# A gate scratch laid out in runs of 1 KB, and gate loads of whole groups into two buffers

## What is computed

```python
        s = jnp.einsum('thik,hink->thin', q, sub_keys.astype(q.dtype)).astype(jnp.float32)
        s_top, i_top = lax.top_k(s, PEER_TOPK)
...
        g = jax.nn.softmax(best_s, axis=-1)
        act = jax.nn.gelu(jnp.einsum('thkd,td->thk', u_tab[eid], tb).astype(jnp.float32), approximate=False)
        return jnp.einsum('thk,thkd->td', (g * act).astype(tb.dtype), v_tab[eid])
```

## Time and profile before

| | |
|---|---|
| median of 3 runs | 2372.03 us (2370.62 to 2372.34) |
| profiled execution, first to last instruction | 2369.0 us |
| TensorE busy | 2339.9 us, 99% |
| VectorE / ScalarE / GpSimd busy | 68% / 33% / 60% |
| DMA | 509.78 MB, mean 215 GB/s; about 320 GB/s from 1380 us on |
| span without what lies around it, against the median | 3.0 us less |

### The profile page before, as it was taken

How to read it: one execution, slowest core, us unless ns; L and a number is a source line. 1 busy time by engine, 2 the same in 40 slices (tenths; PEclk the granted TensorE clock), 3 DMA queues, 4 the chain that set the end, 5 groups by cost and what they waited for, 6 DMA issues and landing times.

```text
span 2369.0 us, 38850 instructions
## 1 busy us (share of the span) xinstructions
PE 2339.9 (99%) x14998; PEld 2182.5 (92%) x14998; DVE 1620.4 (68%) x2679; ACT 770.3 (33%) x1059; POOL 1410.0 (60%) x787
## 2 busy tenths in 40 slices
PE   9999999999999999999999999999999999999998
PEld 8999999987899999999999999999889999999997
DVE  7865444555776244097998988999477777676764
ACT  4442323432232012233343344444333333333332
POOL 5554334432445555447676756877667777777763
PEclk9999999999999999999999999999999999999999
DMA  5223222226753232247677769999988898888872
GB/s 213 79 81 135 98 98 96 100 102 222 263 170 105 87 124 93 86 140 270 230 263 240 251 199 329 320 330 325 337 319 316 318 329 317 321 314 325 319 269 76
DMA packets 207744, 509.78 MB, mean 215 GB/s; under 512 B 15856, under 2 KB 104304, under 8 KB 205168
## 3 DMA queue, kind: packets, MB, share of 16 engines
q1 hardware_dynamic: 115552, 236.75, 31.3%
q10 hardware_dynamic: 55184, 136.80, 15.6%
q0 software_dynamic: 36864, 134.23, 15.2%
HBM read 424.40 MB, written 83.32 MB: 214 GB/s over the span
## 4 chain that ended last, share of the span: by engine, by line
PE 88%; DVE 7%; DMA 2%; ACT 1%; issue 1%; POOL 0%; SPq 0%; DVEq 0%; ACTq 0%; POOLq 0%
PE ps L908 51%; PE ps L644 28%; PE ps L957 3%; DMA cxb<-parked_tiles 1%; DVE prev L1703 1%; PE ps L921 1%; PE ps L821 1%; PE ps L808 1%; PE ps L816 1%; PE ps L841 1%; PE ps L825 1%; DVE n_lo L1819 1%; DMA raw<-units 0%; DMA ug<-rows_u,eid 0%; DVE hu_lo L1532 0%
## 5 line engine op out<-in xcount | busy, mean ns | idle before, releaser
L591 POOL TENSOR_SCALAR w_hi<-raw 128x1024 fp32r<-128x1024 f32 x129 | 139.7, 1083 | 515.5 <-issue 387.4
L618 POOL TENSOR_TENSOR w_lo<-raw,w_hi 128x1024 fp32r<-128x1024 f32 x128 | 316.9, 2476 | 182.1 <-PE ps L908 181.7
L618 POOL TENSOR_TENSOR w_lo<-raw,e_hi 128x1024 fp32r<-128x1024 f32 x128 | 318.6, 2489 | 173.5 <-PE ps L908 166.4
L908 PE MATMUL ps<-g_hi,w_lo 128*128 128x448 f32 x1024 | 375.4, 367 | 0.0
L908 PE MATMUL ps<-p_hi,w_lo 128*128 128x448 f32 x1024 | 375.0, 366 | 0.0
L593 POOL TENSOR_TENSOR w_lo<-raw,w_hi 128x1024 fp32r<-128x1024 f32 x129 | 319.8, 2479 | 10.7
L644 PE MATMUL ps<-h_hi,w_hi 128*128 128x288 f32 (+2 forms) x1216 | 274.1, 307 | 1.3 <-ACT ma L1225 1.1
L644 PE MATMUL ps<-h_lo,w_hi 128*128 128x288 f32 (+2 forms) x1216 | 262.9, 298 | 0.0
L644 PE MATMUL ps<-h_hi,w_lo 128*128 128x288 f32 (+2 forms) x1216 | 262.4, 297 | 0.0
L644 PEld LDWEIGHTS ps<-h_hi,w_hi 128*128 128x128 f32 x1216 | 196.7, 189 | 26.9 <-issue 24.5
L1319 ACT ACTIVATE w_hi<-raw 128x1024 fp32r<-128x1024 f32 x128 | 135.9, 1062 | 238.5 <-PE ps L908 207.0
(11 more groups left out here) (336 smaller groups left out, 5163.5 us busy)
## 6 DMA issues: line engine op xcount, KB each, us to landing
raw<-units SPq DMA_DIRECT2D x385, 512.0 KB, 3.7
gate_scratch<-gt SPq DMA_DIRECT2D x56, 512.0 KB
activation_scratch<-ge ACTq DMA_DIRECT2D x120, 224.0 KB
abuf<-activation_scratch ACTq DMA_DIRECT2D x30, 896.0 KB, 6.2
gbuf<-gate_scratch ACTq DMA_DIRECT2D x30, 896.0 KB, 9.4
prev<-ssm_in ACTq DMA_DIRECT2D x8, 1024.0 KB, 6.8
ssm_s<-prev ACTq DMA_DIRECT2D x8, 1024.0 KB, 4.2
cxb<-parked_tiles ACTq DMA_DIRECT2D x8, 870.0 KB, 6.5
```

Source lines behind the costliest of these rows:

```text
L591: pool.tensor_scalar(w_hi[:, s, :], raw[:, r, :], 1.0, 1.0, ALU.mult, ALU.mult).then_inc(s_whi, 1)
L618: pool.tensor_tensor(w_lo[:, n % 2, :], raw[:, n % RAW, :], e_hi[m % HS_].bitcast(F32), ALU.subtract)\
L908: last = mm(accp[par], w[:, k * P:(k + 1) * P], x_[:, k, t0:t0 + ND], start=k == 0 and i == 0, stop=k == KT - 1 and i == 2)
```

## The change

The scratch becomes `[16, 128, 14, 256]` floats in place of `[32, 128, 14, 128]`: for one partition and one pair of blocks, the gates of all eight tiles of a group lie together, 1 KB in place of 512 bytes. Each store still carries 512 KB. The gates of group 0 come in one load of 1664 KB, and the last pair's copy is one instruction. From group 1 on one DMA of 1792 KB loads a group's gates, to `gbuf0` for even groups and to `gbuf1` for odd ones; `gbuf1` has one half in space that the U half's operands held, so its first load stands behind the last unit of the U half. Later ones stand at the head of a group and wait until VectorE has read the buffer's last group (`s_gr`). Loads of activations stay where they were.

```diff
--- before.py
+++ after.py
@@ -141,7 +141,7 @@
 
 def trunk(nc, xT, x_rows, units, keys, cols, heads, hist_a, hist_s, ssm_in, rows_u, rows_v,
           yT, new_a, new_s, ssm_p, ssm_s):
-    gate_dram = nc.dram_tensor("gate_scratch", [2 * NG, P, NB // 2, GI // 2 * SB], F32).ap()
+    gate_dram = nc.dram_tensor("gate_scratch", [NG, P, NB // 2, GI * SB], F32).ap()
     spill = nc.dram_tensor("parked_tiles", [N_PARK, P, T], F32).ap()
     act_dram = nc.dram_tensor("activation_scratch", [TAIL, P, ND], F32).ap()
     base = ((nc.sbuf_base + 63) // 64) * 64
@@ -319,7 +319,13 @@
         p_lo = [at("p_lo0", R1 + 4 * GI * ND, [P, GI, ND], F32R),
                 at("p_lo1", R_HT + 4 * GI * ND, [P, GI, ND], F32R)]
         abuf = at("abuf", R_XS, [P, 2, GI // 2, ND])
-        gbuf = at("gbuf", R_XS + 4 * GI * ND, [P, 2, NB // 2, GI // 2, SB])
+        gbuf0 = at("gbuf0", R_XS + 8 * GI * ND // 2, [P, NB // 2, GI, SB])
+        G_LOW, G_HIGH = R_HT + 8 * GI * ND, R_XS + 8 * GI * ND
+        G_PART = NB // 4 * GI * SB
+        assert G_LOW + 4 * G_PART <= R_RING and G_HIGH + 4 * G_PART <= R1
+        gbuf1 = at("gbuf1", G_LOW, [P, 2, (G_HIGH - G_LOW) // 4])
+        gate_parts = [gbuf0[:].rearrange("p (a b) i t -> p a b i t", a=2),
+                      gbuf1[:, :, 0:G_PART].rearrange("p a (b i t) -> p a b i t", i=GI, t=SB)]
 
         yo = at("yo", R_XS, [P, KT, TK])
 
@@ -437,6 +443,7 @@
         s_gs = [sem("gates_stored0"), sem("gates_stored1")]
         s_gc = sem("last_gates_copied")
         s_gl = [sem("gates_loaded0"), sem("gates_loaded1")]
+        s_gr = sem("gates_read")
         s_al = [sem("activations_loaded0"), sem("activations_loaded1")]
         s_as = [sem("activations_stored0"), sem("activations_stored1")]
         s_scf = sem("scores_read")
@@ -528,9 +535,9 @@
             def store_gates(B, i):
 
                 sp_.wait_ge(s_gt, 2 * B + 2)
-                gs = slice(2 * NG // GQ * i, 2 * NG // GQ * (i + 1))
+                gs = slice(NG // GQ * i, NG // GQ * (i + 1))
                 sp_.dma_start(gate_dram[gs, :, B].rearrange("g p a -> p g a"),
-                              gt[:, B % 2].rearrange("p (g i) t -> p g (i t)", g=2 * NG)[:, gs]).then_inc(s_gs[B % 2], 16)
+                              gt[:, B % 2].rearrange("p (g i) t -> p g (i t)", g=NG)[:, gs]).then_inc(s_gs[B % 2], 16)
 
             i0, i1 = (U_PEER + M_LEAD) // RAW, -(-(U_PEER + TAIL + GI) // RAW)
             with sp_.Fori(1, i0) as i:
@@ -1399,16 +1406,16 @@
                 act.dma_start(abuf[:, hb], act_dram[bass.ds((g - 1) * GI + hb * (GI // 2), GI // 2)]
                               .rearrange("m p t -> p m t")).then_inc(s_al[hb], 16)
 
-            def load_gates(g, hb, blocks=NB // 2):
-
-                act.dma_start(gbuf[:, hb, 0:blocks].rearrange("p b i t -> p b (i t)"),
-                              gate_dram[bass.ds(g * 2 + hb, 1), :, 0:blocks].rearrange("a p b i -> (a p) b i"))\
-                    .then_inc(s_gl[hb], 16)
-
-            def load_half(g, hb):
-
-                load_acts(g, hb)
-                load_gates(g, hb)
+            def load_first_gates(blocks):
+
+                act.dma_start(gbuf0[:, 0:blocks].rearrange("p b i t -> p b (i t)"), gate_dram[0, :, 0:blocks])\
+                    .then_inc(s_gl[0], 16)
+
+            def load_gates(g, par):
+
+                act.dma_start(gate_parts[par].rearrange("p a b i t -> p a (b i t)"),
+                              gate_dram[bass.ds(g, 1)].rearrange("o p (a b) i -> (o p) a (b i)", a=2))\
+                    .then_inc(s_gl[par], 16)
 
             def hi_part(g, u, par):
                 act.wait_ge(s_pm, g * GI + u + 1)
@@ -1417,14 +1424,13 @@
 
             for u in range(GI):
                 activated(TAIL + u)
-                if u < 2:
+                if u == 0:
                     B = NB // 2 - 1
                     act.wait_ge(s_gs[1 - B % 2], 16 * GQ * ((B + 1) // 2))
                     act.wait_ge(s_gs[B % 2], 16 * GQ * (B // 2))
-                    load_gates(0, u, B)
+                    load_first_gates(B)
                     act.wait_ge(s_gt, NB)
-                    act.activation(gbuf[:, u, B], gt[:, B % 2, u * (GI // 2):(u + 1) * (GI // 2), :], ACT.Copy)\
-                        .then_inc(s_gc, 1)
+                    act.activation(gbuf0[:, B], gt[:, B % 2, 0:GI, :], ACT.Copy).then_inc(s_gc, 1)
                 if u:
                     hi_part(0, u - 1, 0)
                 if u == 5:
@@ -1432,12 +1438,13 @@
                     act.wait_ge(s_as[1], 8 * TAIL)
                     act.wait_ge(s_gs[B % 2], 16 * GQ * (B // 2 + 1))
                     act.wait_ge(s_p, GI // 2)
-                    load_half(1, 0)
+                    load_acts(1, 0)
+            load_gates(1, 1)
             hi_part(0, GI - 1, 0)
             act.wait_ge(s_ud, N_PICK)
             act.activation(dots[:], dots[:], ACT.Gelu).then_inc(s_act, 1)
             act.wait_ge(s_p, GI)
-            load_half(1, 1)
+            load_acts(1, 1)
 
             def group(g, par, load, i=None):
                 g0 = par if i is not None else g
@@ -1446,9 +1453,12 @@
                     if u + 1 < GI:
                         hi_part(g, u + 1, par)
                     expert_hi(NKEYS + (g0 - 1) * GI + u + HS_, i, 4)
+                    if load and u == 0:
+                        act.wait_ge(s_gr, g)
+                        load_gates(g + 1, 1 - par)
                     if load and u % 4 == 2:
                         act.wait_ge(s_p, g * GI + u + 2)
-                        load_half(g + 1, u // 4)
+                        load_acts(g + 1, u // 4)
 
             group(1, 1, True)
             with act.Fori(1, NG // 2 - 1) as i:
@@ -2027,12 +2037,15 @@
                     dve.wait_ge(s_accf[m % 2], m // 2 + 1)
                 elif u % 4 == 0:
                     dve.wait_ge(s_al[u // 4], g * 16)
-                if u % 4 == 0:
-                    dve.wait_ge(s_gl[u // 4], g * 16 + 16)
+                if u == 0:
+                    dve.wait_ge(s_gl[g % 2], g // 2 * 16 + 16)
                     if g == 0:
-                        dve.wait_ge(s_gc, u // 4 + 1)
-                v = abuf[:, u // 4, u % 4, :].rearrange("p (n t) -> p n t", t=SB)
-                tt_(v, v, gbuf[:, u // 4, :, u % 4, :], ALU.mult).then_inc(s_pm, 1)
+                        dve.wait_ge(s_gc, 1)
+                v = abuf[:, u // 4, u % 4, :].rearrange("p (a n t) -> p a n t", a=2, t=SB)
+                tt_(v, v, gate_parts[g % 2][:, :, :, u, :], ALU.mult).then_inc(s_pm, 1)
+                if u == GI - 1:
+                    dve.wait_ge(s_pm, i + 1)
+                    dve.sem_inc(s_gr, 1)
 
             def expert_low(i):
                 g, u = divmod(i, GI)
```

## The result

The changed kernel takes **2385.55 us** (median of 4 runs, 2383.95 to 2385.93) against 2371.32 (4 runs, 2370.41 to 2372.34): ratio 1.0053, 95% interval 1.0039 to 1.0066. It is slower, by 14 us where 3 were forecast, and outside the stated range. In a later measurement, on another chip, the same change came to 1.0028 (1.0017 to 1.0040), 7.5 us (experiment 8). Both intervals say slower; why the two numbers differ is only partly known (experiments 8, 12 and 14). Two executions that ran far longer than all others, 2847.85 us of the kernel before and 7677.64 us of experiment 14, are left out of all numbers here.

The account below looks back on a forecast made before the run. TensorE, busy 99% of the span, was taken as the bound, with 7.2 us at most to regain. The terms -0.3 + 1.1 + 0.7 + 1.6 = +3.1 us on 2372.0 gave 2375.1 us, range 2369.5 to 2379.0 us (8 in 10).

Parts of the forecast that it names:

- Stores, -0.3: Gate stores in 1 KB runs: less DMA time while gates are stored, worth -0.3 us (0 to -0.7).
- I take half of that back: While gates are stored: half of TensorE's 0.7 us loss counted as regained through the longer store runs.
- Pause 1, +1.1: TensorE's wait before unit 124: group 0's one long load makes the weights of m = 125 later, +1.1 us (-1.1 to +2.5).
- Rows 10 show one run per turn: DMA queues: busy queues take turns run by run, so a longer gate load holds up the weights.
- Pause 2, -0.9: First V unit's wait for a low part of group 0: ends at about 1730.6 us in place of 1731.48, -0.9 us.
- Gates of group 1: Head of group 1: one later load of all its gates lands at 1736.4 us; +0.7 us, pause 2 included.
- 9.1 us: Time from issue to landing of group 1's single gate load, from a median of 9.7 us in the trace.
- From there to TensorE's start is the old 3.50 us: Pause 3, third V unit: TensorE starts a fixed 3.50 us after VectorE's first multiplication, at 1739.9 us.
- clearly slower: Rival at the change of halves: gates of both groups land later, 6 us lost, 2378 us; chance 0.21.
- One more half-clock stretch, +1.6: Behind pause 3: TensorE idle for 3.0 us, then one more stretch at half clock, +1.6 us (0 to 1.7).
- The rest, at nothing: V half: gates asked for seven tiles ahead are hidden, and VectorE, 70% busy, absorbs its new wait; 0 us.
- new pauses: Rival in the V half: new pauses once or in every group, 14 pairs at 1 us giving 2386 us; chance 0.06.

Follow-up runs that it names:

- experiment 8: The changed kernel once more, unmodified, on another chip: 2380.47 us, ratio 1.0028 to the kernel before.
- 12: The kernel before again, unchanged, for a second profile of it: 2372.05 us, ratio 0.9993.
- experiment 14: The kernel before with one block of weights of the V half asked for one unit (4.9 us) later: 2375.12 us, ratio 1.0011.
- Experiment 1: The changed kernel with the scratch back in runs of 512 bytes, loads of whole groups and both buffers kept: 2380.63 us, ratio 1.0040.
- experiment 4: The changed kernel without VectorE's wait and count for `s_gr`; ScalarE waits for the group's low parts instead: 2380.95 us, ratio 1.0032.
- Experiments 6: The changed kernel with the gates of group 1 alone loaded in two halves by items, the first with the first activations: 2379.47 us, ratio 1.0034.
- 9: The changed kernel with 512-byte runs and the gates of groups 0 and 1 loaded in halves by items at their old places: 2377.29 us, ratio 1.0013.
- experiments 11: The kernel before with six more VectorE products, whose result nobody reads, once at unit 28 of the V half: 2373.84 us, ratio 1.0001.
- 13: The kernel before with 1.75 MB more read once, into unused space, at unit 12 of the V half: 2372.27 us, ratio 1.0003.
- 17: Experiment 10 with each group's V-half gates in two loads of 896 KB, in the second and fifth unit of the group before: 2373.21 us, ratio 0.9998.
- 10: Experiment 9 with each group's gates of the V half asked for two units later, in the third unit: 2373.53 us, ratio 1.0002.
- 2: The changed kernel with group 1's gates in two loads by blocks, one beside the first activations: 2381.03 us, ratio 1.0032.
- 3: The changed kernel with each group's gates of the V half in two loads of 896 KB: 2381.58 us, ratio 1.0036.

## Why the prediction was wrong, step by step

- *Stores, -0.3.* The queue behaved as worked out: the issues of the last four stores took 3.40 us in place of 9.37, and the DMA share fell by 2 points, some 5.6 us of DMA time over 280 us against 6.7 estimated. TensorE got nothing of it: from the first store to unit 120 it takes 0.1 us longer. The step "I take half of that back" was too kind by 0.3, less than one profile tells.
- *Pause 1, +1.1.* Measured +1.04 us; right, and by the weights, as said. Experiment 1 adds that the longer runs take 1.0 us off it (4.22 against 3.23), twice the 0.5 of the sum, and by the second path: TensorE waits there for GpSimd's low part, behind the gates. "Rows 10 show one run per turn" says more than they do; they show equal counts over 2 us.
- *Pause 2, -0.9.* Measured -0.90; right in kind and size.
- ***Gates of group 1: failed.*** With pause 2 the term was to be +0.7 and came to -0.90 + 4.41 = +3.5. The landing was mis-sized, 12.0 us in place of 9.1 (in experiment 8 the gates landed after 10.4). The "9.1 us" took the median of all gate loads, most of them in the V half, where the DMA engines are 88% busy, for a load at the change of halves, where they are 93% busy, and full while this one was under way (384 GB/s from 1730.13 to 1742.10 us). "The end of this stretch is less crowded than most of it" had no row behind it, and was wrong. But the step that decides is "From there to TensorE's start is the old 3.50 us". It was 3.84 us here, 4.71 in experiment 4 (gates after 9.6 us, a pause of 6.21) and 5.65 in experiment 1 (after 8.7 us, a pause of 5.70): a landing as forecast would have left nearly all of the pause. The sum added lateness to a fixed 3.50 us; the runs show late gates that push the multiplications under GpSimd's subtraction. The rival "clearly slower" had the late gates and its turning point (1738 us) right: less the 2.3 us by which this trace is late at unit 120, VectorE had them at 1739.8. It too counted time for time, 2.5 us for this pause. Experiments 6 and 9 show the cause by removing it.
- *One more half-clock stretch, +1.6.* It came, 6.8 us long, its first 3.1 us in the pause; what is left over in the sum is 6.08 - 1.04 - 3.51 = 1.5 us. Right.
- ***The rest, at nothing: failed.*** The V half lost 4.6 us in the profiled execution and, by experiment 8, nothing in another. The step looked for waits of TensorE for weights ("more than the 9.7 us that two units cover") and found none. It took VectorE's 70% as 30% of reserve. The reserve is gone as soon as a wait well inside those 9.7 us (6.62 to 9.20 in the traces) shifts VectorE under GpSimd; that late weights alone can do it, experiment 14 shows. "Against it: weights late there 30 times, by up to 6.1 us, without a pause" was true, 0.5 us short of where the second profile of before fell in. The rival "new pauses" with its 0.06 named the place and not the mechanism.

What stays open: how often each kernel falls into the slow pattern, and with it how the 14.2 us of the first measurement and the 7.5 of the second divide beyond the 5 to 6 us of the change of halves that both traces share. The first profile adds 4.6 us of the V half, the second 3.2 us at the end of the kernel, and both some 2 us ahead of the change.

## What to carry to other kernels

Fewer and longer loads cost their reader the time of the whole: a load whose first quarter is needed at once should be cut along the order of use, and the layout in memory has to allow that cut in long runs. Take the landing time of a moved load from the place to which it moves, at that place's DMA share, and not from a median over the kernel. Then ask what the reader runs into when it starts late: here the neighbour's next instruction made one step of some 4 us out of it. Before calling an engine's idle 30% a reserve, look at what its instructions would take if they fell against its neighbour's, and judge a stretch that has two patterns only from more than one profile.

## What the runs showed of the hardware

- Two stable patterns of one program: a VectorE product of 128x448 with both operands in SBUF takes 0.63 us free, 0.97 when it meets the end of GpSimd's 2.4 us subtraction, up to 2.83 when it begins with or just behind its start; VectorE at 70% or 95%, TensorE 4.1 to 5.7 us longer over 574.
- Equal counts of packets between busy queues over 2 us, whatever their size, from 512 bytes (192 to 209) to 13 KB (48, 48, 47). The Trainium skill, "DMA: Bandwidth & Descriptors", section Queues, rings and completion order, has a turn last for a packet of 9 to 17 descriptors; these counts neither show such a grouping nor how long a turn is.
- The clock: in all seven pauses of 5.68 to 6.21 us a stretch of 6.8 us at 0.50 (1.2 of 2.4 GHz) began, in those of 8.2 and 8.3 us one of 10.2 and of 6.8. Pauses of 2.1 to 2.3 us were followed by 3.4 us of it in the first profile of before and in experiments 11, 12 and 13, and by none in 9, 14 and 17 (in 10 only behind the second, of 2.38); those of 3.29 (8) and 3.31 us (2) by none, others of 3.2 to 3.3 us by 3.4 (change, 4) and 6.8 (3). The length of the pause alone doesn't decide it.
